# A fused transformer kernel: attention scores with 128 rows throughout, transfers spaced beside the RWKV heads, and five places reordered

## The reference, cut to what matters

```python
# first block
h = rms_norm(x); proj = h @ w_in                                # 1024 -> 2496
x = x + concat([mla(proj), retention(proj)]) @ w_out            # mla: 4 heads, keys 128 + 64 rotary
x = x + memory_cross_attention(rms_norm(x), rms_norm(mem))
x = x + hierarchical_moe(rms_norm(x))                           # 32 experts, 2 of 8 in one of 4 groups
# second block
x = x + (concat([forgetting_attention(h), pooled(h)]) @ w_out)  # 8 heads of 64, logits + cum_q - cum_k
x = x + swiglu(rms_norm(x))
x = x + rwkv7_time_mix(rms_norm(x)) @ w_o                       # 16 heads of 64, low-rank w, a, g
x = x + swiglu(rms_norm(x))
```

## Time and profile before

| what | value |
|---|---|
| median of 3 runs | 1426.78 us (1425.82 to 1427.17) |
| the profiled execution: its own time | 1429.99 us |
| its span, first to last instruction | 1428.2 us |
| mean granted TensorE clock | 0.917 of full speed |
| busy: TensorE, its weight loads | 1243.0 us (87%), 888.1 us (62%) |
| busy: VectorE, ScalarE, GpSimd | 731.8 us (51%), 248.9 us (17%), 95.3 us (7%) |
| transferred | 247.27 MB, mean 173 GB/s |
| chain that ended last | TensorE 78%, DMA 9%, VectorE 6%, ScalarE 3%, "issue" 2% |

### The profile page before, as it was taken

One profiled execution on the slowest core, in us unless ns is written; L12 is line 12 of the kernel. 1 busy time (PEld: TensorE's weight loads), 2 busy tenths in 40 slices (PEclk: granted clock), 3 DMA queues, 4 the chain that ended last, 5 costly groups with the idle time before them and its releaser, 6 DMA issues.

```text
span 1428.2 us, 20792 instructions
## 1 busy us (share of the span) xinstructions
PE 1243.0 (87%) x8985; PEld 888.1 (62%) x8985; DVE 731.8 (51%) x1157; ACT 248.9 (17%) x428; POOL 95.3 (7%) x84
## 2 busy tenths in 40 slices
PE   4999999868676567898899999977999887999998
PEld 3864544546333332685648888864769885588886
DVE  4545522223111112634258777675587465877774
ACT  4412202120000002412210000134430200100000
POOL 2000000000000000130000000000020332100000
PEclk9998999878888778896599999998999999999999
DMA  9553134065999999330185554034310302865500
GB/s 337 201 177 117 59 117 154 24 269 231 399 395 418 408 393 392 112 121 1 51 288 169 195 181 148 16 92 149 143 37 4 111 15 89 294 193 190 178 30 30
DMA packets 106340, 247.27 MB, mean 173 GB/s; under 512 B 8114, under 2 KB 56257, under 8 KB 93827
## 3 DMA queue, kind: packets, MB, share of 16 engines
q1 hardware_dynamic: 106052, 245.71, 47.2%
q0 software_dynamic: 144, 0.15, 0.0%
q10 hardware_dynamic: 46, 0.01, 0.0%
HBM read 244.80 MB, written 1.05 MB: 172 GB/s over the span
## 4 chain that ended last, share of the span: by engine, by line
PE 78%; DMA 9%; DVE 6%; ACT 3%; issue 2%; SPq 1%; POOL 0%; DVEq 0%; ACTq 0%
PE bank L468 13%; PE bank L469 13%; PE bank L470 13%; DMA ring_w<-expert_w_gate 8%; PE bank L336 8%; PE bank L322 6%; PE bank L2302 4%; PE bank L1315 3%; PE bank L1330 2%; SPq L292 1%; PE bank L1878 1%; PE bank L1880 1%; PE bank L436 1%; PE bank L2208 1%; PE bank L2196 1%
## 5 line engine op out<-in xcount | busy, mean ns | idle before, releaser
L468 PE MATMUL bank<-work_rounded,work_rounded 128*128 128x512 f32 (+2 forms) x704 | 281.1, 399 | 18.8 <-DVE ring_w_rounded L499 10.8
L470 PE MATMUL bank<-work_rounded,work_rounded 128*128 128x512 f32 (+2 forms) x704 | 277.0, 394 | 0.0
L469 PE MATMUL bank<-ring_w_rounded,work_rounded 128*128 128x512 f32 (+2 forms) x576 | 229.8, 399 | 0.0
L468 PEld LDWEIGHTS bank<-work_rounded,work_rounded 128*128 128x128 f32 x704 | 134.7, 191 | 50.6 <-DVE ring_w_rounded L499 11.4
L470 PEld LDWEIGHTS bank<-work_rounded,work_rounded 128*128 128x128 f32 x704 | 134.3, 191 | 29.0
L469 PEld LDWEIGHTS bank<-ring_w_rounded,work_rounded 128*128 128x128 f32 x576 | 111.8, 194 | 23.4
L336 PE MATMUL bank<-ring_w,work 128*128 128x512 f32 x256 | 113.5, 601 | 2.6 <-ACT work L1121 1.4
L1653 DVE TENSOR_TENSOR ring_w_rounded<-ring_w,work_rounded 128x1024 fp32r<-128x1024 f32 x84 | 102.9, 1225 | 2.9
L1315 PE MATMUL bank<-ring_w,work 128*32 128x256 f32 x768 | 66.6, 432 | 34.7 <-DMA ring_w<-expert_w_gate 33.7
L1214 ACT ACTIVATE work<-bank 128x256 f32<-128x256 f32 x52 | 20.1, 386 | 405.7 <-PE bank L470 340.4
L336 PEld LDWEIGHTS bank<-ring_w,work 128*128 128x128 f32 x256 | 48.5, 193 | 60.9 <-issue 57.6
(11 more groups left out here) (442 smaller groups left out, 1849.2 us busy)
## 6 DMA issues: line engine op xcount, KB each, us to landing
ring_w<-expert_w_gate SPq DMA_DIRECT2D x26, 1024.0 KB, 14.0
ring_w<-expert_w_up SPq DMA_DIRECT2D x22, 1024.0 KB, 20.0
ring_w<-ffn_w_down SPq DMA_DIRECT2D x22, 1024.0 KB, 5.0
work<-expert_w_down SPq DMA_DIRECT2D x20, 1024.0 KB, 8.9
ring_w<-expert_w_down SPq DMA_DIRECT2D x12, 1024.0 KB, 11.2
work<-ffn_w_gate SPq DMA_DIRECT2D x12, 1024.0 KB, 5.4
work<-ffn_w_up SPq DMA_DIRECT2D x12, 1024.0 KB, 8.0
work<-expert_w_up SPq DMA_DIRECT2D x10, 1024.0 KB, 11.4
```

Source lines behind the costliest of these rows:

```text
L468: nc.tensor.matmul(out, lhsT[0], rhs[0], start=first, stop=False)
L469: nc.tensor.matmul(out, lhsT[0], rhs[1], start=False, stop=False)
L470: return nc.tensor.matmul(out, lhsT[1], rhs[0], start=False, stop=last)
```

## The change

Seven things are changed. (1) Both score matmuls now take 128 rows: rows 64 to 127 of `ropeT` and rows 8 to 127 of `ncumT` are set to zero by GpSimd first. (2) Each unit of `w_ro` after the first waits for a level of the second half of the heads, and slots 4 and 5 of the last SwiGLU wait for `yS.3.1`. (3) The opening transposes both tiles first, ScalarE cuts the first weight unit between the two norms, VectorE orders the low parts ahead of tile 1's input; low parts are made in two halves, each signalled, here and for `w_fin`. (4) The router's counts get a bank of their own and their copies stand behind the eight `Sel`. (5) `down`, the copy to `ysb` and `scatter` are signalled by half, `scatter` goes by tiles first, and the next norm waits for one tile at a time; a wait behind the overflow block is gone. (6) VectorE makes the high part of `w_rr`'s input, and ScalarE's high part of `w_rr.0.4` stands behind the copy of the low product `la`. (7) The four 128-row matmuls of `g` come before the four 32-row ones.

```diff
         moved = {r: sem(f"moved_{r}") for r in RINGS}
+        MOVES = {"Y": 2}
+        moves = lambda ring, n: n * MOVES.get(ring, 1)
...
                 if name.startswith("w_ro."):
                     await_moved(sp, "HT1.0.1")
+                    step = ("0.0", "0.4", "1.0", "1.4").index(name[5:])
+                    if step:
+                        peek(sp, f"dY{step - 1}.1.1")
...
-            dve.wait_ge(sem("w_high"), COUNT_FROM[name] + n + 1)
-            nc.vector.tensor_tensor(unit_view(whole, True), unit_view(whole), part_high(name, n).bitcast(F32),
-                                    ALU.subtract).then_inc(sem("w_low"), 1)
+            dve.wait_ge(sem("w_high"), HIGHS_FROM[name] + n + 1)
+            kt = views[whole][2]
+            for p_ in (slice(0, kt // 2), slice(kt // 2, kt)):
+                nc.vector.tensor_tensor(unit_view(whole, True)[:, p_], unit_view(whole)[:, p_],
+                                        part_high(name, n)[:, p_].bitcast(F32), ALU.subtract).then_inc(sem("w_low"), 1)
...
-            norm_pe(pe, u, tiles=(0,))
+            norm_pe(pe, u, tiles=range(T) if both_first else (0,))
...
-                if (c, t) == (1, 0):
+                if (c, t) == (1, 0) and not both_first:
...
-                    pe.wait_ge(sem("w_low"), COUNT_FROM[name] + n + 1)
...
+                        if (k - k0) % (kt // 2) == 0 and t == 0:
+                            pe.wait_ge(sem("w_low"), COUNT_FROM[name] + 2 * n + 1 + (k - k0) // (kt // 2))
...
-            rounded_linear(pe, "a", "w_in", IN1, "AD")
+            rounded_linear(pe, "a", "w_in", IN1, "AD", True)
...
-                    mm = nc.tensor.matmul(ps[:, lo:hi], ropeT[0:RD, 0, h, tq * P:(tq + 1) * P],
-                                          ropeT[0:RD, 1, h, 0:n], start=False, stop=True)
+                    mm = nc.tensor.matmul(ps[:, lo:hi], ropeT[:, 0, h, tq * P:(tq + 1) * P],
+                                          ropeT[:, 1, h, 0:n], start=False, stop=True)
...
-            norm_act(act, "a", X)
-            for n in range(4):
+            norm_act(act, "a", X, ready=lambda t: part_high_act(act, "w_in", 0) if t else None)
+            for n in range(1, 4):
                 part_high_act(act, "w_in", n)
...
+            peek(pool, "w_in.4.1")
+            nc.gpsimd.memset(ropeT[RD:P], 0.0).then_inc(sem("zeros"), 1)
+            pool.wait_ge(sem("zeros"), 1)
...
-            norm_split_dve(dve, "a", "attn_norm_g", 0)
-            part_low_dve(dve, "w_in", 0)
-            part_low_dve(dve, "w_in", 1)
-            norm_split_dve(dve, "a", "attn_norm_g", 1)
+            for half in range(2):
+                norm_split_dve(dve, "a", "attn_norm_g", 0, halves=(half,))
+                part_low_dve(dve, "w_in", half)
             part_low_dve(dve, "w_in", 2)
             part_low_dve(dve, "w_in", 3)
+            norm_split_dve(dve, "a", "attn_norm_g", 1)
...
-            nc.tensor.matmul(ps[:, NE:2 * NE], C("strictP"), picked[:, 1], start=False, stop=True)
-            nc.tensor.matmul(ps[:, 2 * NE:3 * NE], C("ones"), picked[:, 0], start=True, stop=False)
-            nc.tensor.matmul(ps[:, 2 * NE:3 * NE], C("ones"), picked[:, 1], start=False, stop=True).then_inc(full["D"], 1)
-            drained(pe, "D", "A")
+            nc.tensor.matmul(ps[:, NE:2 * NE], C("strictP"), picked[:, 1], start=False, stop=True).then_inc(full["D"], 1)
+            ps = fill(pe, "D", "count")
+            nc.tensor.matmul(ps[:, 0:NE], C("ones"), picked[:, 0], start=True, stop=False)
+            nc.tensor.matmul(ps[:, 0:NE], C("ones"), picked[:, 1], start=False, stop=True).then_inc(full["D"], 1)
+            drained(pe, "A")
...
-            act.wait_ge(sem("down_moe"), q + 1)
...
             for c in range(2):
-                mm = nc.scalar.copy(ysb[:, c * 512:(c + 1) * 512], RINGS["Y"][0][c][:, :])
-            mm.then_inc(moved["Y"], 1)
+                act.wait_ge(sem("down_moe"), 2 * q + c + 1)
+                nc.scalar.copy(ysb[:, c * 512:(c + 1) * 512], RINGS["Y"][0][c][:, :]).then_inc(moved["Y"], 1)
...
-                    mm = nc.tensor.matmul(ps[:, lo:hi], C("sel")[0:FH, h * P:(h + 1) * P], ncumT[0:FH, 0:hi - lo],
+                    mm = nc.tensor.matmul(ps[:, lo:hi], C("sel")[:, h * P:(h + 1) * P], ncumT[:, 0:hi - lo],
...
-            for t in range(T):
-                for c in range(2):
-                    ps = fill(pe, "A", f"g.{c}.{t}")
...
+            gates = [(t, c, fill(pe, "A", f"g.{c}.{t}")) for t in range(T) for c in range(2)]
+            for t, c, ps in gates:
+                nc.tensor.matmul(ps[:, :], glow[:, 0, t * P:(t + 1) * P], w2[:, 0, c * 512:(c + 1) * 512],
+                                 start=True, stop=False)
+            for t, c, ps in gates:
+                nc.tensor.matmul(ps[:, :], glow[0:GL - P, 1, t * P:(t + 1) * P],
+                                 w2[0:GL - P, 1, c * 512:(c + 1) * 512], start=False, stop=True).then_inc(full["A"], 1)
...
+                if name == "la":
+                    high_act(act, "w_rr", 0, 4)
...
-                    x_high_act("w_rr", xi[1], 7)
-                    high_act(act, "w_rr", 0, 4)
...
             shift(2)
+            shift(3)
+            dve.wait_ge(sem("xi"), 7)
+            L(V.tensor_copy(x_high["w_rr"], xi[1]))
+            V.tensor_tensor(x_low["w_rr"], xi[1], x_high["w_rr"].bitcast(F32), ALU.subtract).then_inc(sem("x_low"), 1)
             low_dve(dve, "w_rr", 0, 0)
-            shift(3)
-            x_low_dve("w_rr", xi[1], 5)
             low_dve(dve, "w_rr", 0, 4)
...
-        slot_fence = {4: "UG.1.3", 5: "UG.1.3", 6: "yS.3.1", 7: "yS.3.1"}
+        slot_fence = {4: "yS.3.1", 5: "yS.3.1", 6: "yS.3.1", 7: "yS.3.1"}
```

More of the change, by code:

```diff
@@ L182, in fill @@
             if n >= size:
-                pe.wait_ge(moved[ring], n - size + 1)
+                pe.wait_ge(moved[ring], moves(ring, n - size + 1))
             return RINGS[ring][n % size]
@@ L206, in await_moved @@
             for ring, n in need.items():
-                eng.wait_ge(moved[ring], n)
+                eng.wait_ge(moved[ring], moves(ring, n))
         def drained(eng, *rings):
@@ L497, in part_low_dve, with norm_split_dve @@
             whole = f"{name}.{c}.{k0}"
-            dve.wait_ge(sem("w_high"), COUNT_FROM[name] + n + 1)
-            nc.vector.tensor_tensor(unit_view(whole, True), unit_view(whole), part_high(name, n).bitcast(F32),
-                                    ALU.subtract).then_inc(sem("w_low"), 1)
-        def norm_split_dve(dve, u, gain, t, gi=0):
+            dve.wait_ge(sem("w_high"), HIGHS_FROM[name] + n + 1)
[3 more added lines that the diff above has]
+                                        part_high(name, n)[:, p_].bitcast(F32), ALU.subtract).then_inc(sem("w_low"), 1)
+        def norm_split_dve(dve, u, gain, t, gi=0, halves=range(2)):
             tok = slice(t * P, (t + 1) * P)
-            for half in range(2):
+            for half in halves:
                 h4 = slice(half * 4, half * 4 + 4)
@@ L721, in mixA_pe @@
             await_moved(pe, "ropeT.1.0", "ropeT.1.1")
+            pe.wait_ge(sem("zeros"), 1)
             for h in range(H):
@@ L1323, in down_quad_pe @@
             for j in range(EPQ):
-                released[unit_at[f"moe.d.{q}.{j}"]] = (sem("down_moe"), q + 1)
+                released[unit_at[f"moe.d.{q}.{j}"]] = (sem("down_moe"), 2 * q + 2)
             await_moved(pe, f"moe.T.{q}")
@@ L1377, in scatter @@
             def scatter(q):
-                await_moved(pe, f"y.{q}", f"selT.{q}")
-                for c in range(2):
-                    for t in range(T):
+                await_moved(pe, f"selT.{q}")
+                for t in range(T):
+                    for c in range(2):
+                        if t == 0:
+                            pe.wait_ge(moved["Y"], 2 * q + c + 1)
                         ps = fill(pe, "Z", f"x.{q}.{c}.{t}")
@@ L1545, in moe_dve @@
                 V.tensor_tensor(quad(Sel, q), slots_of(key, q), each, ALU.is_equal).then_inc(sem("selected"), 1)
+            V.tensor_copy(place_of, by_tile).then_inc(moved["D"], 1)
+            ps = take(dve, "D", "count")
+            V.tensor_copy(count, ps[:, 0:NE]).then_inc(moved["D"], 1)
             dve.wait_ge(sem("gexp"), 2)
@@ L1581, in moe_dve @@
                 V.tensor_tensor(quad(SelG, q), quad(Sel, q), slots_of(gate, q), ALU.mult).then_inc(sem("gated"), 1)
-            await_moved(dve, "rank")
+            await_moved(dve, "rank", "count")
             L(V.tensor_scalar(late_gate, place_of, float(CAP), None, ALU.is_ge))
@@ L1914, in fox_act, with ready @@
             part_high_act(act, "w_fin", 1)
-            if "C" in phases:
-                await_moved(act, f"x.{NQ - 1}.1.1")
-                if "O" in phases:
-                    act.wait_ge(sem("overflow_added"), 1)
-            def second_pair(t):
+            def ready(t):
                 if t:
@@ L1922, in second_pair @@
                     part_high_act(act, "w_fin", 3)
```

(18 more changed lines are left out.)

39 lines of the change are left out of this document (20 added, 19 removed).

## The result

The changed kernel takes 1377.07 us (median of four runs, 1372.87 to 1378.45) and the one before 1426.97: a ratio of 0.9639, 95% interval 0.9608 to 0.9670. I had forecast 1370 with a range of 1357 to 1389. The profiled execution took 1377.43 with a span of 1375.6, 52.6 less than the 1428.2 of before; my sum was 57.0.

The account below looks back on a forecast made before the run. TensorE, with 78% of the chain, was taken as the bound. Eight parts summed to 57.0 us off 1429.99, giving 1373.0; less 3.2 for the median this was told as 1370, range 1357 to 1389.

Parts of the forecast that it names:

- Part 1: Opening: both tiles transposed first and low parts ready earlier end TensorE's waits and cold matmuls; -8.0 us (-6 to -9.5).
- Parts 2 and 4: MLA and forgetting attention scores: all matmuls over 128 rows run faster and the clock mostly recovers; -8.5 and -15.5 us.
- rival that rows don't matter: MLA and forgetting attention scores: filling rows with zeros saves nothing, total 1394 us; chance 0.05.
- Part 3: Router and experts' end: earlier gather and weight stream at most about 1.1 us, signalling by halves 0.5; -1.6 us (-0.6 to -2.5).
- Part 5: Low-rank products: `la`'s copy ahead of `w_rr`'s input work removes waits and cold matmuls; -12.5 us (-10 to -13.5).
- Part 6: Gate `g`: grouping matmuls of like rows saves 0.19 us on each of four pairs, and a restart; -1.0 us (0 to -1.6).
- Part 7: Second heads: spacing the 4 MB `w_ro` burst removes TensorE's 2.89 us stop and slow stretch; -4.5 us, down to -1.5.
- the stops move: Stops are not the bulk transfers', or later units meet the next fetch: 9.9 us lost, total 1380; chance 0.13.
- Part 8: Heads of tokens 128 on: issuing the first gate and up weights later removes the 4.41 us stop; -5.4 us (-3.5 to -6.7).

Follow-up runs that it names:

- e2: Changed kernel with g's second matmul over 128 rows (zero-filled), in pairs with the first: 1374.00 us, ratio 0.9624 to the kernel before.
- e3: Changed kernel with every unit of `w_ro` issued one level later: 1375.70 us, ratio 0.9635 to the kernel before.
- e9: Changed kernel with the router's counts in the rank's bank again and their copies ahead of the `Sel`: 1378.54 us, ratio 0.9655 to the kernel before.
- e4: Changed kernel with score matmuls over 64 and 8 rows again, zeroing left in: 1404.23 us, ratio 0.9824 to the kernel before.
- e5: As e4, but each head's second tile starts with the short matmul, giving two changes of row count instead of four: 1398.42 us, ratio 0.9794.
- e7: Changed kernel with the low-rank products' former order on ScalarE and VectorE: 1386.70 us, ratio 0.9725 to the kernel before.
- e6: Changed kernel with slots 4 and 5 of the last SwiGLU (2 MB) issued at their old place: 1382.05 us, ratio 0.9685 to the kernel before.

## Why the prediction was right or wrong

- **Part 1** right (-8.0, measured -8.5): the low parts were ready in time. Chunk 0 began 0.7 later than put and took 7.2 instead of 8.3, since the clock was whole sooner.
- **Parts 2 and 4** right in mechanism and near in size. MLA's scores took 6.96 us and not 5.2, as the clock was still low in the first of them, while the linear behind gave its 1.6; in e2, e3 and e9, where the clock was whole from the first score, they took 5.3. The other scores took 12.25 for my 14.5, from the latency that I had added for VectorE's copies: it did not show. Eight heads at 2.6, all at half clock, would take 20.8 us, between the 29.4 of before and the 12.25: about half of what these scores gave is the changes of row count, the other half the clock, which stays at 0.50 in e4 and e5 and gets whole here. What I had read as "beside one of other row count" e5 makes exact. The rival that rows don't matter is out.
- **Part 3**, -1.6 forecast, -0.4 between two single profiles, is not settled: from the last addition of the cross attention to that of the experts 263.1 us passed before and 257.2 to 262.5 in the twelve profiles of the changed kernel and its edits (e9: 259.6). The gather's 1.1 is real (e9). "The expert weights' stream behind starts sooner by it" was wrong for the first set of transfers, which is issued at 266.54, 36 us ahead of the gather; the next set does start 1.1 sooner (53.7 us behind the first, in e9 54.8). The halves' 0.5 at the end did not come: ScalarE idles for 5.55 to 5.85 us in those twelve profiles instead of 5.12.
- **Part 5** right: -12.5, measured -12.7, e7 13.0 at its place. What the sum lacked is that `w_rv` then starts with 1.6 us more at half clock.
- **Part 6** wrong in sign: -1.0 forecast, +2.2 measured. I had priced the changes of row count (the pairs' 8.42 us became 7.86) and not what four short-row products do to the clock; the transposes went from 3.7 to 6.4.
- **Part 7** wrong: -4.5 forecast, +0.2 measured. The step that failed is that the stop belongs to the 4 MB burst; one MB is enough to hold the instruction packet up (e3). Its low end (the first MB alone makes it) was the case, and that end was still too good, because I had counted the other three units, now spread over later levels, as free. The rival "the stops move" is right here and wrong for part 8.
- **Part 8** right: -5.4, measured -5.1, e6 4.05 at its place and 5.2 in the span.
- **Not in the sum at all**: the clock in the cross attention (-4.6) and behind `w_rv`'s start (+1.6), where no instruction was changed. The parts that I had forecast gave 49.6 of their 57.0; the other 3.0 of the 52.6 are these two. That they closed part of the gap is luck, and the 4.6 are 2.0 in five other profiles.
- **The median**: I took off 3.2 us because the profiled execution of before lay that far above its median. The changed kernel's lay 0.4 above. Of the 7.1 between 1370 (1369.8 unrounded) and 1377.07, 4.4 are the sum (1377.43 against 1373.0) and 2.8 are this. The kernel before ran in 1423.71 to 1432.43 over all its runs, so 3.2 off a median of three was no size to count on. The upper end of the range, 1389, is that of all low ends together, not of most of them.

The rule that I had set against parts 7 and 8, from the section "Instruction fetch mechanics" of "Runtime: NRT & Kernel Launch" in the Trainium skill, says that the sequencer fetches instructions with a DMA queue of its own, in blocks of 16 KiB. The trace agrees: packets of 16 KB on q8, and one in each stop or just ahead of it. That a crossing is mostly hidden holds for most packets, and not for one that a bulk transfer delays: 2.50 us with 1 MB, 4.58 with 2 MB (e6). For ScalarE's 5.12 us the section's other case fits, a taken branch to code outside its two fetched blocks: another instruction queue (q14) has a packet from 565.52 to 565.86 before and from 544.40 to 544.74 after, each 1.47 us ahead of ScalarE's next copy. By the sections "LDWEIGHTS (loading the stationary operand)" and "Why this matters for your kernels" of the Trainium skill's "TensorE: Matmul & The Clock Gate" alone part 4 would have given nothing. It gave 17.5 us, so the measurement decides; e5 shows where both meet: the short matmul isn't slower, the change of row count costs.

## What to carry to other kernels

Count the changes of row count between neighbouring matmuls, not the matmuls with few rows: fill the short ones with zeros where the operand is cheap to zero. Never price an order on TensorE without asking what it does to the granted clock behind it. When TensorE stops for nothing that the profile shows, look for a packet of the instruction queue in the stop or just ahead of it and for the bulk transfer ahead of it, and move that transfer by itself before spacing the rest: a later transfer can meet a later fetch, and the same cure gave 5 us at one place and nothing at another. Read a stage in several profiles before laying a few microseconds to an edit.

## What the runs showed of the hardware

- A change of row count costs 0.30 us at half clock (e4 against e5) and 0.19 at full clock (1.05 a pair, e2: 0.86).
- TensorE at 6.00 busy of 6.00 us can be at half clock (after, 1016 to 1022): four products of 32 rows stand ahead of it. With 128 rows in their place the clock stays whole (e2), and once it did so with the 32 rows too (e7).
- The same program ended its expert stage, with the DMA engines busy for 0.96 to 0.97, at 539.3 us in one execution (397 GB/s) and at 543.8 in another (392 GB/s). What sets the rate was not found.
- A TensorE stop without a releaser ends 1.19 to 1.61 us behind the landing of a 16 KB instruction packet (67 stops in 13 profiles). One MB arriving delayed such a packet so that TensorE stood for 2.5 us; 2 MB held it for 4.41 before and 4.58 in e6.
